# Expert rows of a routed MoE picked on TensorE chunk by chunk, instead of through DRAM

## The reference, cut to what matters

```python
def mem_kv(mem, w_kv):                        # 256 memory tokens, once per layer
    k, v = jnp.split(mem @ w_kv, 2, axis=-1)
def moe_tokens(x, w_router, r_bias, wg, wu, wd):
    ...                                       # idx: the two experts of a token, w: their weights
    combine = jnp.sum(one_hot(idx, 16) * w[..., None], axis=1)
    h = silu(einsum('td,edf->tef', x, wg)) * einsum('td,edf->tef', x, wu)
    h = h * combine[..., None]
    return einsum('tef,efd->td', h, wd)
xp = layer_norm(ALPHA * xp + moe(xp, ...), ...)
```

## Time and profile before

| | us |
|---|---|
| median of 3 runs | 1506.80 (1497.52 to 1507.07) |
| the profiled execution, its own time | 1495.84 |
| its span | 1494.2 |
| expert loop of layer 0, first gate and up to last rows out | 520.35 to 795.70 |
| expert loop of layer 1 | 1167.25 to 1445.12 |

### The profile page before, as it was taken

One profiled execution on the slowest core, in us unless ns is written; L12 is line 12 of the kernel. 1 busy time (PEld: TensorE's weight loads), 2 busy tenths in 40 slices (PEclk: granted clock), 3 DMA queues, 4 the chain that ended last, 5 costly groups with the idle time before them and its releaser, 6 DMA issues.

```text
span 1494.2 us, 23953 instructions
## 1 busy us (share of the span) xinstructions
PE 1125.8 (75%) x9604; PEld 766.7 (51%) x9605; DVE 429.3 (29%) x1055; ACT 249.5 (17%) x502; POOL 184.2 (12%) x265
## 2 busy tenths in 40 slices
PE   6998879999899668544869897989884568547660
PEld 4676555767477534222544675767463435223330
DVE  0124737133314212111323105124232223112235
ACT  1016421123204200000101212013121101000011
POOL 2016970000001200000001000000004000000022
PEclk9999999999999889776989898999995889777885
DMA  9647789435753689999998431316744698999921
GB/s 331 225 141 222 237 302 385 173 113 191 289 193 132 247 305 397 395 394 397 361 357 299 139 114 60 113 57 226 281 169 176 229 395 306 394 395 396 354 58 55
DMA packets 158374, 373.75 MB, mean 250 GB/s; under 512 B 7463, under 2 KB 7607, under 8 KB 158298
## 3 DMA queue, kind: packets, MB, share of 16 engines
q1 hardware_dynamic: 148226, 340.15, 62.8%
q0 software_dynamic: 9936, 32.40, 6.2%
q10 hardware_dynamic: 144, 0.25, 0.1%
HBM read 350.10 MB, written 23.10 MB: 250 GB/s over the span
## 4 chain that ended last, share of the span: by engine, by line
PE 54%; DMA 26%; DVE 8%; issue 4%; SPq 3%; ACT 2%; POOL 1%; DVEq 0%; ACTq 0%; POOLq 0%
PE acc L683 34%; DMA ring<-in_w_exp_up 17%; PE psS L683 9%; DMA by_slot<-zT 4%; PE psV L683 4%; DMA zT<-by_slot 2%; PE acc L977 2%; DVE zT L1732 1%; SPq L610 1%; PE acc L786 1%; DMA ring<-in_w_in_even 1%; DMA arena<-by_slot,arena 1%; DMA ring<-in_w_xkv 1%; SPq L611 1%; PE acc L1138 1%
## 5 line engine op out<-in xcount | busy, mean ns | idle before, releaser
L683 PE MATMUL psS<-ring,zT 128*32 128x256 f32 x3328 | 236.0, 446 | 161.1 <-DMA ring<-in_w_exp_up 144.7
L683 PEld LDWEIGHTS psS<-ring,zT 128*32 128x32 f32 x3328 | 124.6, 128 | 254.0 <-issue 212.5
L683 PE MATMUL acc<-xT,ring 128*128 128x288 f32 x768 | 193.3, 415 | 8.2 <-ACT xT L1897 4.2
L683 PEld LDWEIGHTS acc<-xT,ring 128*128 128x128 f32 x768 | 149.4, 195 | 51.4 <-issue 9.4
L683 PE MATMUL acc<-mixT,ring 128*128 128x288 f32 x512 | 126.8, 410 | 2.7 <-DVE mixT L1621 1.6
L1732 DVE COPY zT<-psV 32x256 f32<-32x256 f32 x208 | 86.9, 418 | 102.4 <-DMA by_slot<-zT 73.8
L1723 DVE TENSOR_TENSOR zT<-zT,psS 64x256 f32<-64x256 f32 x52 | 22.1, 425 | 326.2 <-ACT zT L1983 326.0
L683 PEld LDWEIGHTS acc<-mixT,ring 128*128 128x128 f32 x512 | 98.1, 192 | 30.8 <-DVE mixT L1621 2.0
L683 PE MATMUL psV<-ring,zT 128*32 128x256 f32 x1664 | 101.8, 385 | 11.3 <-DVE zT L1727 11.3
L1261 ACT ACTIVATE arena<-acc 128x1024 f32<-128x1024 f32 (+7 forms) x116 | 81.7, 728 | 153.3 <-PE acc L1138 46.6
L1983 ACT ACTIVATE zT<-psS 64x256 f32<-64x256 f32 x52 | 19.6, 376 | 488.4 <-PE psS L683 488.4
(11 more groups left out here) (328 smaller groups left out, 1160.3 us busy)
## 6 DMA issues: line engine op xcount, KB each, us to landing
ring<-in_w_exp_gate SPq DMA_DIRECT2D x32, 2048.0 KB, 16.0
ring<-in_w_exp_up SPq DMA_DIRECT2D x32, 2048.0 KB, 21.2
ring<-in_w_exp_down SPq DMA_DIRECT2D x32, 2048.0 KB, 14.1
ring<-in_cache_k SPq DMA_DIRECT2D x64, 256.0 KB, 3.1
ring<-in_cache_v SPq DMA_DIRECT2D x64, 256.0 KB, 3.0
ring<-in_w_xkv SPq DMA_DIRECT2D x8, 2048.0 KB, 16.0
ring<-in_cache_mem_k SPq DMA_DIRECT2D x32, 512.0 KB, 5.4
ring<-in_cache_mem_v SPq DMA_DIRECT2D x32, 512.0 KB, 5.3
```

Source lines behind the costliest of these rows:

```text
L683: return pe.matmul(out, lhsT, rhs, start=first, stop=last)
```

## The change

The rows of a chunk are no longer sent through DRAM. `XTOK`'s copies now go to `XSPLIT`, token by width with the width dealt in eight parts (element 8m + k lies in part k). For each chunk DVE makes a one-hot matrix `G` (tokens by 32 slots) from `ROW`, and PE multiplies it with `XSPLIT` (`fetch`, 12 products of 256 columns in four column groups). ACT copies the result (`split`), PE turns it (`turn_x`), and ACT copies it to `XS` (`take`). The scatter, the five loads, the 18 turned tiles and `XE` are gone. `by_slot` stays for the output rows.

Gate and up are read with rows of 16 KB and down with rows of 8 KB, by letting a partition hold neighbouring rows of the matrix.

The memory projection of layer 1 is dealt out anew: ahead of layer 0's loop only key tile 1 is left; key tiles 2 and 3 and value tiles 0 and 1 follow the loop; value tiles 2 and 3 go into `cross(1)`, as in layer 0. The unit order moves with them. POOL scales x to `XTOK` out of `XSPLIT` at once, and waits for `slots_zero`, `out_mem` and `slots_ready` later; ACT's and DVE's waits for `out_mem` ahead of the loop are gone or stand after it.

```diff
@@ unit_order
-        if l == 0:
-            u += [("xkv", 0, 3)]
+        u += [("xkv", l, 3)]
...
-            u += [("xkv", l + 1, n) for n in range(2)]
+            u += [("xkv", l + 1, 0)]
         u += [("moe", l, n) for n in range(3 * NE)]
-            u += [("xkv", l + 1, n) for n in range(2, 4)]
+            u += [("xkv", l + 1, 1), ("xkv", l + 1, 2)]
@@ sync
-                        k = 8 if j % 3 < 2 else 4
-                        sp.dma_start(slot(u + j).rearrange("p (k n) -> p k n", k=k),
-                                     w[l, bass.ds(e, 1)].rearrange("a (k p) n -> p (a k) n", p=P))\
+                        if j % 3 < 2:
+                            sp.dma_start(slot(u + j), w[l, bass.ds(e, 1)].rearrange("a (p k) n -> p (a k n)", k=8))\
...
+                            sp.dma_start(slot(u + j).rearrange("p (h n) -> p h n", h=2),
+                                         w[l, bass.ds(e, 1)].rearrange("a (h p j) n -> p (a h) (j n)", h=2, j=2))\
-                sp.wait_ge(scattered, 16 * 6 * (l + 1))
-                for n in range(3):
-                    sp.dma_start(XROWS[n], by_slot[...]).then_inc(rows_in[n], 16)
...
@@ tensor
+            def fetch(S, c, bank, later):
+                pe.wait_ge(S.picked, c + 1)
+                if later:
+                    pe.wait_ge(S.split, c)
+                for t, r in enumerate(rows_of):
+                    for q in range(4):
+                        last = mm(bank[32 * q:32 * q + 32, 0:256], G[0:r, t, :],
+                                  XSPLIT[0:r, t, 2 * q:2 * q + 2, :].rearrange("p k m -> p (k m)"), t == 0, t == 2)
+                last.then_inc(S.fetched, 1)
+
+            def turn_x(S, c, bank):
+                pe.wait_ge(S.split, c + 1)
+                for j in range(2):
+                    last = pe.transpose(bank[:, P * j:P * j + P], XR[:, P * j:P * j + P], ident)
+                last.then_inc(S.x_turned, 1)
...
-                    memory_keys(l + 1, (1, 2, 3))
-                for i in range(2 * NXT):
...
+                    memory_keys(l + 1, (1,))
...
                     with pe.If(extra > 0):
                         with pe.Fori(0, extra) as j:
                             c = first + j
+                            fetch(S, c + 2, to_split, True)
                             gate_and_up(S, c + 1, Wg, Wu)
+                            turn_x(S, c + 2, to_turn)
                             down(S, c, Wd)
                             turn_h(S, c + 1)
                     c = first + extra
                     mark(to_mark, gate_up_used)
                     if into is not None:
                         Ng, Nu, _ = matrices(e + 1)
+                        fetch(S, c + 2, to_split, True)
                         expert_in(e + 1, 0, into), expert_in(e + 1, 1, into)
                         gate_and_up(S, c + 1, Ng, Nu)
+                        turn_x(S, c + 2, to_turn)
                     down(S, c, Wd)
...
+                fetch(S, 0, to_split, False)
+                turn_x(S, 0, to_turn)
+                fetch(S, 1, to_split, True)
                 expert_in(0, 0, 0), expert_in(0, 1, 0)
                 gate_and_up(S, 0, Wg, Wu)
+                turn_x(S, 1, to_turn)
                 turn_h(S, 0)
...
-                    memory_values(l + 1)
+                    memory_keys(l + 1, (2, 3))
+                    memory_values(l + 1, (0, 1))
@@ vector
+                def pick(c, later):
+                    if later:
+                        dve.wait_ge(S.seq, c)
+                    dve.tensor_tensor(PAIR, ROW..., SLOTNO..., ALU.is_equal).then_inc(S.match, 1)   # 128 x 192
+                    dve.wait_ge(S.match, c + 1)
+                    if later:
+                        dve.wait_ge(S.fetched, c)
+                    dve.tensor_tensor(G, PAIR[:, 0:3, :], PAIR[:, 3:6, :], ALU.add).then_inc(S.picked, 1)
+                    dve.tensor_scalar(SLOTNO, SLOTNO, float(CAP), None, ALU.add).then_inc(S.seq, 1)
...
                 hidden_turned(1)
+                pick(3, True)
                 with dve.Fori(1, last) as c:
                     hidden(c + 1)
                     dve.wait_ge(S.stored, 16 * c)
                     rows_out(c)
                     hidden_turned(c + 1)
+                    pick(c + 3, True)
@@ scalar
                 with act.Fori(0, last) as c:
-                    take(c + 1, slot_rows(c + 1))
+                    split(c + 2)
                     act.wait_ge(S.h, c + 1)
                     silu(c + 1)
+                    take(c + 2)
@@ gpsimd
-                        pool.indirect_dma_start(by_slot, ..., XTOK[0:r, t, :], None).then_inc(scattered, 16)
```

More of the change, by code:

```diff
@@ L382, in build @@
         YS = work[0:CAP, 896:1920]
+        XR = work[:, 1920:2176]
+        G = work[:, 2176:2272].rearrange("p (t m) -> p t m", t=3)
         W4 = arena[0:DS, 10496:10528].rearrange("p (g t) -> p g t", g=8)
@@ L1127, in experts @@
                 if l + 1 < DEPTH:
-                    memory_keys(l + 1, (1, 2, 3))
-                for i in range(2 * NXT):
[L1131 to L1143, removed]
+                    memory_keys(l + 1, (1,))
+                for i in range(6):
+                    evacuated(pe, f"xtok{l}", i)
+                evacuated(pe, f"rank{l}", 0)
                 S = chunks[l]
@@ L1702, in _ @@
                 dve.tensor_copy(LASTI, LASTF).then_inc(steps_ready, 1)
-                dve.wait_ge(out_mem, 32 * (l + 1))
-                cm["xg"](l)
-                full(dve, f"xg{l}", 2 * NXT - 1)
                 dve.memset(H[0:64, :], 0.0)
+                pick(1, True)
+                pick(2, True)
+                dve.tensor_copy(IDX, ROW).then_inc(slots_ready, 1)
                 link(dve.tensor_tensor(tmp, sc, top, ALU.mult))
@@ L1712, in _ @@
                                        mx.unsqueeze(2).to_broadcast([P, 3, NE]), ALU.mult))
-                for pick in range(2):
-                    link(dve.tensor_tensor(PICK, POS, ROW[:, pick, :].unsqueeze(2).to_broadcast([P, 3, NE]), ALU.is_equal))
+                for nth in range(2):
+                    link(dve.tensor_tensor(PICK, POS, ROW[:, nth, :].unsqueeze(2).to_broadcast([P, 3, NE]), ALU.is_equal))
                     link(dve.tensor_tensor(PICK, PICK, COMB, ALU.mult))
-                    link(dve.tensor_reduce(WT[:, pick, :], PICK, X, ALU.add))
-                S = chunks[l]
+                    link(dve.tensor_reduce(WT[:, nth, :], PICK, X, ALU.add))
                 def hidden(c):
@@ L1970, in _, with split, take @@
                 if l + 1 < DEPTH:
-                    memory_keys(l + 1, (1, 2, 3))
-                act.wait_ge(out_mem, 32 * (l + 1))
-                cm["xg"](l)
+                    memory_keys(l + 1, (1,))
                 S = chunks[l]
-                def take(c, at):
-                    act.activation(XS, XE[:, :, at], ACT.Copy).then_inc(S.rows, 1)
+                def split(c):
+                    act.wait_ge(S.fetched, c + 1)
+                    act.activation(XR, acc[:, spare_bank(l, 0), 0:256], ACT.Copy).then_inc(S.split, 1)
+                def take(c):
+                    act.wait_ge(S.x_turned, c + 1)
+                    act.activation(XS.rearrange("p (q j) m -> p j q m", q=4),
+                                   acc[:, spare_bank(l, 1), 0:256].rearrange("p (j q m) -> p j q m", j=2, q=4), ACT.Copy)\
+                        .then_inc(S.rows, 1)
                 def silu(c):
@@ L2090, in _ @@
                     evacuated(pool, f"xtok{l}", i)
-                pool.wait_ge(slots_zero, 16 * NXT)
-                pool.wait_ge(slots_ready, l + 1)
-                for t, r in enumerate(rows_of):
-                    for pick in range(2):
-                        pool.indirect_dma_start(by_slot, bass.IndirectOffsetOnAxis(IDX[0:r, pick, t:t + 1], 0),
-                                                XTOK[0:r, t, :], None).then_inc(scattered, 16)
                 if l + 1 == DEPTH:
@@ L2111, in _ @@
                 pool.wait_ge(all_stored, l + 1)
+                pool.wait_ge(out_mem, 32 * (l + 1))
+                pool.wait_ge(slots_ready, l + 1)
                 for t, r in enumerate(rows_of):
```

107 lines of the change are left out of this document (56 added, 51 removed).

## The result

The changed kernel takes 1600.6 us (median of four runs, 1593.6 to 1620.1) against 1502.2 (median of four) for the kernel before. One of its runs fell in a slower state of the chip; without it the ratio is 1.065, 95% interval 1.056 to 1.073. The forecast was 1524, at most 1552: the sign and the mechanism are right, the size is not. The profiled execution has a span of 1591.7 us, 97.5 more than the 1494.2 of before, and that difference is what has to be found.

What follows compares the result with a forecast made beforehand. PE (54%) and DMA (26%) led the chain of waits: weights bound one-chunk experts, PE the last stretch. Removed way -61.6, loops +75.2, memory projection +8.1 make +22 on 1502: 1524 us, range 1480 to 1552.

Steps and rivals of the forecast that it cites:

- The bound and the removed way: Ahead of both expert loops: dropping the way through DRAM saves 34.2 us in layer 0, 27.4 in layer 1, together 61.6.
- The wait: In each chunk, PE's next fetch waits for DVE's pick behind rows out: 2.84 us from down's end to fetch.
- P: Time of one chunk in experts of several chunks: 11.3 us, bounds 9.9 and 11.9, counted 35 times over both loops.
- From fetch to the end of down: PE's part of each chunk: fetch 1.29, gate and up 3.48, turn 0.37, down 1.91, together 7.05 us.
- Where it cost: Gate and up after PE's idle time: the lower clock costs 1.7 us, in 8 of 10 chunks, adding 1.4 per chunk.
- The ring: Each chunk's repeating chain, fetch to down's end (7.05 us), then rows out and pick to the next fetch (2.84 us).
- Experts of one chunk: In the loops' one-chunk stretches the weights bind; longer weight rows make an expert 15.05 us instead of 16.28.
- The memory projection: Value tiles 2 and 3 moved into cross(1) cost 8.1 us; the other moved tiles cost nothing.
- The clock holds: Rival, chance 0.19: PE's idle in the chunks doesn't lower its clock; a chunk takes 9.9 to 10.2, total 1475 to 1486.
- It doesn't serialise: Rival, chance 0.06: fetch finds its pick ready; a chunk takes 7.4 or 7.6 us, total about 1394.
- Long rows aren't faster: Rival, chance 0.12: rows of 16 and 8 KB bring the expert weights no gain; +14 us, total 1538.
- stores wait by the number of rows: Rival, chance 0.05: output stores wait by the count of weight rows ahead; a chunk takes 21 us, total over 1750.

Runs made afterwards that it cites:

- experiment 5: The changed kernel with DVE's pick ahead of rows out and POOL's scaling of x moved behind slots_ready; 1458.2 us, ratio 0.969 to the kernel before.
- experiment 4: The kernel before with only the memory projection of layer 1 dealt out anew; 1497.7 us, ratio 0.996.
- Experiment 1: The changed kernel with DVE's pick(c + 3) moved to the head of its iteration, ahead of hidden and rows out; 1460.6 us, ratio 0.971 to the kernel before.
- pick first: The kernel of Experiment 1: the changed kernel with DVE's pick moved ahead of rows out; run twice, 1460.6 and 1460.9 us.
- experiment 2: The changed kernel, pick left late, with 40, 20 or 10 products of constants behind every turn_h in the loop; 1615.7, 1538.9 and 1530.7 us.
- experiment 3: The kernel before with only the expert weights' layout changed, to rows of 16 and 8 KB; 1471.2 us, ratio 0.980.

## Why the prediction was right in kind and wrong in size

**The bound and the removed way: right.** The prelude (slots known to first gate and up) of layer 0 lost 34.5 us (34.2 forecast), that of layer 1 23.5 (27.4). Of the 4 missing some 3 are two fetches at the lower clock (2.94 each where I had 1.3), and 1 is DVE's operations beside POOL's scaling, which I had costed at nothing but a late store: with the scaling moved (experiment 5) this prelude takes 7.8 us for 8.7, with both fetches still at 2.94. Some 8 of the 34 are not the DRAM way's but SP's queue behind key tiles 2 and 3 (experiment 4); the sum is right, the reason I gave for those tiles ("lay hidden under the scatter") was wrong.

**The wait: right.** Fetch waits for a pick behind rows out, 2.86 to 2.88 us against 2.84. Experiment 1 takes it away without changing an instruction.

**P: the step that failed.** The prediction counted 35 chunks at P = 11.3; measured 12.79 on average in the 33 between the first and last DVE multiplication of those stretches. 35 x 1.49 = 52, and that is nearly all of the loops' miss: from first gate and up to last rows out they took 320.8 + 362.8 = 683.6 us against 628.4. The whole forecast missed by some 76, so this is two thirds of it. Two terms of P were mis-sized.

- "From fetch to the end of down: 1.29 + 3.48 + 0.37 + 1.91 = 7.05." Measured at the full clock 1.64 + 3.59 + 0.37 + 1.91 = 7.51. Fetch was priced at down's pace, 54 ns an instruction; it takes 68. PE's weight loads pause for 0.41 us ahead of its last eight instructions (weights of 32 rows by 32, at 727.36) and again ahead of gate and up (727.92), where the shape changes back. P at the full clock is 10.37, not 9.9: 35 x 0.47 = 16 us.
- "Where it cost ... 1.7 us. I put it at 8 periods in 10: P = 9.9 + 1.4." Measured 12.79 - 10.37 = 2.42: 36 us. The share of periods was about right (30 of 33 are slow), the price was not. The 1.7 us came from the earlier trace rows, where nothing but gate and up stood behind the idle time. In the changed kernel fetch stands there first: in the dear case it takes 2.93 for 1.64 and gate and up 5.55 for 3.59. My upper bound of 11.9 ("always") took over the same 1.7, and so the range could not hold the truth. The ring then repeats it, since each chunk brings the idle time again. The Trainium skill, TensorE: Matmul & The Clock Gate, "A second HAM failure mode: psum-queue depth-cycling", tells of such a kernel, whose brief idles between groups of products make the clock swing between its levels; this trace agrees, with 0.77 to 0.84 in those stretches.

**Experts of one chunk: right.** Their two stretches took 101.9 and 85.9 us against 100.6 and 85.5; the experts that the weights bind take some 15.1 us, at 427 GB/s. In layer 1 the first ones ran at the ring's 13.6 us, with weights in store from the experts of three chunks; that this sum comes out the same is partly luck.

**The memory projection: its size about right in place (+5.9 for +8.1), its sign wrong alone.** Alone it gains, because the 8 us that it takes off layer 0's prelude outweigh the tiles; in the changed kernel that gain is already inside the 34.5. Between the loops 16.9 us were added instead of 8.1. Beside the tiles' 5.9, another 5.9 came from 48 small products (L687, 13.75 us for 7.84) at a granted clock of 0.50 for 1.00. They did so in three of the seven profiles of the changed code, partly in two more, and in none of the three of the kernel before and its variants. The two profiles of pick first, one and the same kernel, have 7.84 and 13.75: it differs from execution to execution. What decides it stays open. The rest is small: the gather 2.2 later, the transposes ahead of the rank 5.38 for 4.22, DVE's operations up to L1717 beside POOL's scaling.

**Chance.** 8.9 us of the profiled difference come from the clock in unchanged work early on; medians over runs carry less of it.

**The rivals.** "The clock holds" is refuted by the trace, and its time was too low as well: experiment 2 with 10 products is its case (the clock holds, the wait stays). At P = 10.37 the sum would be 1502 - 61.6 + (232.9 + 363.0 - 553.2) + 8.1 = 1491; measured 1531. "It doesn't serialise" is the case of experiment 1, which takes 1461, not 1394. Both miss the same way: the shorter a chunk, the more stretches the weights bind again, which a formula in P alone leaves out. In experiment 1 the DMA share is 0.99 even among experts of two chunks (546 to 571); experiment 2 with 10 products has its 18.2 us ahead of layer 0's last expert. "Long rows aren't faster" and "stores wait by the number of rows" are refuted by experiment 3.

## What to carry to other kernels

In a loop of several engines, write down for each engine what stands ahead of the instruction that another engine waits for; a helper for two chunks ahead must not stand behind the work of the oldest one. Where an idle time on TensorE recurs in each round, ask what would stand right behind it and price that at the lower clock (here fetch and gate and up, 3.25 us), not only the one operation in which a trace has shown the cost. When a kernel's edits are several, time each alone: here the weight rows alone were worth -34 us and the dealing of the memory projection alone -7, and with fetching by products the three together came out at +98, because of an order that costs nothing to change. In the better order they come to -45, of which the long rows alone make 34. Against experiment 3, which has the same rows, pick first saves 57.7 us in the two preludes (74.7 to 17.0) and pays 41.3 in the loops (492.9 to 534.2): some 70% of what the way through DRAM cost comes back as a price on the chunks.

## What the runs showed of the hardware

- Products that compute nothing made a kernel 70 us faster (1530.7 for 1600.6): with 1.03 us of idle time left in each chunk the granted clock was 0.95 to 1.00 in the stretches of several chunks, with 2.4 us it averaged 0.77 to 0.84 in those shown above.
- A chunk of the same instructions takes 10.4 to 10.8, about 12.0 or 13.4 to 13.6 us (3, 11 and 19 of 33) and nothing between.
- Operations of DVE on 32 to 192 elements a partition took 1.07 to 2.35 us beside POOL's scaling of 128 x 1024, and 0.17 to 0.36 without it. The Trainium skill, SBUF — State Buffer, "SBUF: two separate sides", names a pair of ports that only one of VectorE and GpSimd holds at a time, for a whole instruction; the slow operations agree with it in kind, but others beside them (L1730, two inputs, 0.26 us in the same stretch) ran at their usual time, so which pairs collide is not settled here.
- Rows of 16 and 8 KB carried 427 GB/s where rows of 2 and 4 KB carried 395, and the stores beside them landed 0.4 us later (median 5.6 against 5.2).
